# Layer 1's FFN with the turn of each conditioning slot's sums one tile later in the order

## The reference

```python
mod_x = (s_c @ w_mod[l] + b_mod[l])[:, None, :]
sa_x, ca_x, ga_x, sf_x, cf_x, gf_x = jnp.split(mod_x, 6, axis=-1)
...
f_x = _conv_ffn(h_x * (1.0 + cf_x) + sf_x, ffn_w_up[l], ffn_conv_w[l], ffn_conv_b[l], ffn_w_down[l])
h_x = _layer_norm(ALPHA * h_x + gf_x * f_x, ln_g[l, 1], ln_b[l, 1])
...
def _conv_ffn(h, w_up, conv_w, conv_b, w_down):
    u = h @ w_up
    up = jnp.pad(u, ((0, 0), (1, 1), (0, 0)))
    u = up[:, :-2] * conv_w[0] + up[:, 1:-1] * conv_w[1] + up[:, 2:] * conv_w[2] + conv_b
    a, v = jnp.split(u, 2, axis=-1)
    return (jax.nn.silu(a) * v) @ w_down
```

## Time and profile before

| | us |
|---|---|
| median of 3 runs | 2008.89 |
| lowest and highest of them | 2004.92, 2014.71 |
| the profiled execution's own time | 2010.19 |
| its span, first to last instruction | 2008.3 |
| PE busy in the span | 1878.0 |
| DVE busy | 1319.2 |
| POOL busy | 926.3 |
| ACT busy | 889.2 |

### The profile page before, as it was taken

One profiled execution on the slowest core, in us unless ns is written; L12 is line 12 of the kernel. 1 busy time (PEld: TensorE's weight loads), 2 busy tenths in 40 slices (PEclk: granted clock), 3 DMA queues, 4 the chain that ended last, 5 costly groups with the idle time before them and its releaser, 6 DMA issues.

```text
span 2008.3 us, 32378 instructions
## 1 busy us (share of the span) xinstructions
PE 1878.0 (94%) x12286; PEld 1589.9 (79%) x12286; DVE 1319.2 (66%) x2566; ACT 889.2 (44%) x1909; POOL 926.3 (46%) x770
## 2 busy tenths in 40 slices
PE   7899899999999999999999989989899888988997
PEld 4788798767778888888888878888777767877886
DVE  3248999676675977888625366989576754255545
ACT  3224678577443222222433344648377333323542
POOL 3145467111344345554633345766153544754743
PEclk9899799999999999999999999999999999999999
DMA  8563001310111322332221131011401122322321
GB/s 357 201 245 112 22 22 33 110 44 2 64 42 63 122 89 105 126 105 105 84 74 63 42 116 52 34 43 54 152 2 44 63 84 105 105 105 84 126 98 71
DMA packets 29546, 179.38 MB, mean 89 GB/s; under 512 B 3024, under 2 KB 6224, under 8 KB 10320
## 3 DMA queue, kind: packets, MB, share of 16 engines
q1 hardware_dynamic: 22976, 158.16, 21.7%
q10 hardware_dynamic: 6416, 19.14, 2.6%
HBM read 172.05 MB, written 5.24 MB: 88 GB/s over the span
## 4 chain that ended last, share of the span: by engine, by line
PE 66%; DVE 22%; issue 4%; ACT 3%; POOL 2%; DMA 2%; ACTq 1%; DVEq 0%; SPq 0%; POOLq 0%
PE PS L1276 20%; PE PS L1171 18%; PE PS L887 8%; DVE W L1706 6%; PE PS L881 4%; PE PS L1109 3%; PE PS L1133 3%; PE PS L1020 2%; DMA WR<-in_weights 2%; DVE W L1704 2%; PE PS L1093 2%; DVE U L1941 2%; DVE W L2050 1%; PE PS L816 1%; PE PS L1099 1%
## 5 line engine op out<-in xcount | busy, mean ns | idle before, releaser
L1276 PE MATMUL PS<-XH,WS 128*128 128x512 f32 x2016 | 545.3, 357 | 0.9 <-POOL WS L2437 0.9
L1276 PEld LDWEIGHTS PS<-XH,WS 128*128 128x128 f32 x2016 | 361.5, 191 | 55.7 <-POOL WS L2437 1.3
L1276 PE MATMUL PS<-XL,WS 128*128 128x512 f32 x1008 | 359.3, 356 | 0.0
L2437 POOL TENSOR_TENSOR WS<-WR,WS 128x1024 fp32r<-128x1024 f32 x88 | 213.4, 2425 | 311.6 <-ACT WS L1578 311.4
L1642 ACT ACTIVATE W<-PS,PR 128x768 f32<-128x768 f32 (+1 forms) x88 | 78.0, 886 | 440.6 <-PE PS L1276 379.8
L2265 DVE SCALAR_TENSOR_TENSOR W<-PS,PR,W 128x511 f32<-128x511 f32 (+1 forms) x132 | 82.9, 656 | 215.3 <-ACT W L1642 215.3
L1276 PEld LDWEIGHTS PS<-XL,WS 128*128 128x128 f32 x1008 | 192.5, 191 | 26.8
L887 PE MATMUL PS<-EU,XH 128*128 128x256 f32 x624 | 190.1, 305 | 5.6 <-issue 4.6
L2373 POOL TENSOR_TENSOR WL<-WR,EU 128x512 fp32r<-128x512 f32 x96 | 129.5, 1375 | 128.7 <-ACT EU L1333 128.7
L887 PE MATMUL PS<-WL,XH 128*128 128x256 f32 x624 | 182.0, 292 | 0.0
L887 PE MATMUL PS<-EU,HL 128*128 128x256 f32 x624 | 182.0, 292 | 0.0
(11 more groups left out here) (220 smaller groups left out, 4191.7 us busy)
## 6 DMA issues: line engine op xcount, KB each, us to landing
WR<-in_weights SPq DMA_DIRECT2D x128, 1024.0 KB, 4.7
U<-in_weights SPq DMA_DIRECT2D x16, 1024.0 KB, 7.8
U<-in_bias ACTq DMA_DIRECT2D x2, 1792.0 KB, 10.1
H<-in_x SPq DMA_DIRECT2D x1, 2048.0 KB, 7.9
H<-in_x ACTq DMA_DIRECT2D x1, 2048.0 KB, 14.9
U<-in_ln_rows ACTq DMA_DIRECT2D x2, 1024.0 KB, 4.6
WR<-in_weights SPq DMA_DIRECT2D x4, 512.0 KB, 3.7
kept<-H ACTq DMA_DIRECT2D x4, 512.0 KB, 2.6
```

The source lines that it names most:

```text
L1276: mm = pe.matmul(PS[u.pos][:, lo:hi], w[:, part, k, :], src[:, k, lo:hi], start=(k == 0 and src is xh3 and part == 0), stop=(k == KT - 1 a ...
L2437: pool.tensor_tensor(ws5[:, u.c % 2, 1], half_slot(u), ws5[:, u.c % 2, 0], ALU.subtract).then_inc(w_low, 1)
```

## The change

In `ups`, after it is filled, each conditioning entry of layer 1 moves two places on, so that it stands behind both halves of the next tile.

```diff
@@ -627,6 +627,9 @@
                 u = Job()
                 u.kind, u.l, u.j, u.key = "mod", int(key[2] >= LATE), key[2], key
                 ups.append(u)
+        for n in range(len(ups) - 3, -1, -1):
+            if ups[n].kind == "mod" and ups[n].l > 0:
+                ups.insert(n + 2, ups.pop(n))
         n_m = 24 + EARLY
         c = 0
         for u in ups:
```

## The result

The changed kernel takes 1981.58 us (median of four runs, 1976.77 to 1987.43) against 2008.35 for the kernel before on the same chip: a ratio of 0.9864, interval 0.9827 to 0.9902. Two later comparisons of the same pair, with more runs of the kernel before, give 0.9877 (0.9858 to 0.9897) and 0.9877 (0.9861 to 0.9893), which is 24.7 us. The profiled execution took 1987.43 us with a span of 1985.6, 22.7 less than before.

What follows compares the result with a forecast made beforehand. PE was taken as the bound, busy 94% of the span, with time to win only at its stalls: 32.9 us removed less 10.2 of new stops gives 22.7, so 2008.89 - 22.7 = 1986.2 us, range 1982 to 1994.

Steps and rivals of the forecast that it cites:

- The stalls and their slow restarts: Layer 1's up side: PE's four waits for DVE's accumulation, 25.7 us, plus 7.2 us of slow matmuls behind them, go.
- (3,0): First half of tile 3: PE waits for weights whose transfer starts after POOL's low part of (2,1); 1.8 us lost.
- (4,0): First half of tile 4: its weights take slot 20's place, given back after the accumulation; PE loses 1.2 us.
- (5,0): First half of tile 5: weights ready at 1658.4, just when PE gets there; nothing lost, or a few tenths.
- (6,0): First half of tile 6: weights wait for slot 21's place, freed after a 14.8 us accumulation; PE loses 2.1 us.
- The unknown cost of the accumulation: Slot 21's accumulation on DVE may be a microsecond shorter with fewer POOL instructions beside it; 2 us more gain.
- The clock behind the short stops: PE's six stops of about 2 us: no clock loss taken; upper end 9 to 13 us of slow restarts.
- rival 1: PE's clock falls in the new short stops; gain about 15.5 us, 1993 us; chance 0.15.
- Rival 2: Weights land later as two transfers share engines; 5 to 9 us lost, about 1993 us; chance 0.08.
- Rivals 3 and 4: 3: PE waits as long elsewhere for DVE, 2009 us, chance 0.03; 4: clock stays low between stops, 2034 us, 0.02.
- The rest of the span is the same: Outside layer 1's up stage, the span stays the same to a microsecond or two; nothing after takes the gain back.

Runs made afterwards that it cites:

- Experiment 7: Kernel before, with POOL's low part of the weights of layer 1's tiles 3, 5, 16 and 18 cut from 1024 to 64 columns: 1980.66 us, ratio 0.9862.
- experiment 3: The change with each conditioning entry moved one place on instead of two: ratio 0.9891 to the kernel before, stage 244.2 us.
- 8: The changed kernel with three more 512-column products on POOL for each of layer 1's tiles 2 and 15: ratio 0.9943 to the kernel before, stage 253.4 us.
- experiment 9: The change with each entry moved one place on instead of two, run again for a second profile: ratio 0.9898 to the kernel before, stage 245.0 us.

## Why the prediction was right or wrong

The forecast was 1986.2 us, with a range from 1982.0 to 1994.0. The first result, 1981.6, lies just under it; the two repetitions, 1983.2 and 1984.5, lie inside. The mechanism was right; one loss in the sum was too large and the range had too little room below. Against the 26.7 us of the stage the gain was forecast 4.0 too small; taken from the forecast's base of 2008.89 that makes 1982.2, inside the range by 0.2, so the scatter of four runs decides on which side of its lower end their median falls.

- *The stalls and their slow restarts, 32.9 us gone.* Right. The wait's row is gone, and the clock is 1.00 in every stretch of the stage in all three profiles of the change. A little was forgotten: the transposes had cost 0.74 us each at the low clock and cost 0.35 now (1673.87 to 1674.22), 1.6 us more for four.
- *(3,0), 1.8 us lost.* Right: 1.76 idle; by the distance of the matmuls it is 2.1 (1614.94 and 96 matmuls make 1636.7, the next starts at 1638.80).
- *(4,0), 1.2 us lost.* Right: 1.36 idle, 1.6 by distance.
- *(5,0), nothing, or a few tenths.* Right: no idle time there, and its first matmuls come 0.2 us late.
- ***(6,0), 2.1 us lost. Wrong, and this is the step that failed.*** It took the accumulation of slot 21 at the 14.8 us of slot 20. It took 10.1, with one low part and one product of POOL beside it (3.9 us) where slot 20's had three and two (9.4 us before). It began about 1 us later than forecast, so slot 21's place was free 3.6 us sooner than in the sum (1664.30 less the 4.0 by which the stage starts later, against 1663.9). With the sum's 8.4 us from there to ready weights tile 6 was ready at 1672.7, and PE came to it at 1674.22. Twice 2.1 makes 4.2 us. With all of this the sum is 32.9 + 1.6 - 2 x 3.7 = 27.1 for a measured stage of 26.7.
- *The unknown cost of the accumulation.* I had named it as open, "a microsecond shorter" with fewer of POOL's instructions beside it. It was 4.7. The rows could have told more: in 14.8 us are 16 instructions, of which a median one takes 0.48 (the trace of before, L1706: 472/484/2645 ns), so about 7 us were something else, and POOL was busy for 9.4 us of them all. Experiment 7 showed that it was POOL. The rows of this case agree with a rule of the Trainium skill, SBUF — State Buffer, in the section on who interferes with whom, that VectorE, in an instruction with two inputs in SBUF, and GpSimd share a pair of ports that the one to start first keeps for its whole instruction: the longest instruction of the accumulation, 2.6 to 2.7 us, is one of POOL's 2.4 and a little. I didn't weigh it.
- *The clock behind the short stops.* No loss taken, and none seen in the change: three profiles with stops of 1.3 to 1.9 us have clock 1.00 throughout. The reason given was weaker than it read, though: the first case of the earlier trace rows has no unbroken matmuls right ahead of its 2.31 us, but two matmuls and, before them, a stop of 0.59 (1253.10 us). But rival 1 is real. It came in experiments 3, 8 and 9, once or twice a profile, behind stops of 1.87, 1.87 and 3.21, and 2.53 us; where it could be measured it took 1.7 us ((3,0) in experiment 3 ran 7.2 us, in experiment 9 5.5). The change had four such stops in each of three profiles and no fall, which doesn't prove that none will come.
- *Rival 2, later weights.* Not seen in the change, where (4,0) came when order of issue said; a part of it, 1.4 us a transfer, seen in experiment 3. *Rivals 3 and 4.* Not seen.
- *The rest of the span is the same.* The stage's gain isn't given back after it: from the first down products to the end of the span go 129.7 us before (2008.3 - 1878.60) and 129.8 now (1985.6 - 1855.84). Ahead of it the profiles differ by up to 10 us with no change at all, which the range should have had room for on both sides. A gain of 27 with the noise of four runs reaches below 1982 easily.

## What to carry to other kernels

Where an in-order engine stops for a product that it need not yet have, count what stands behind it and put as much of it ahead as the wait is long; then look at once for what the stall had covered, since here a better place for the weights was worth 0 us before the change and 8 after it. Don't carry an instruction's duration from one place to another without its neighbours: read the fastest, the median and the slowest of its kind, and ask which engine was at work during the slow ones. When a kernel's spans scatter by more than the effect, measure the stage between two rows that the scatter doesn't reach.

## What the runs showed of the hardware

DVE's accumulation in SBUF slows down with POOL's work beside it, over four stretches by about 0.8 us for 1 us: 9.8 us with 3.6 us of POOL, 16.1 with 11.7. That much of a stall that the profile puts down to DVE being POOL's doing I had not expected. DVE's taps, that read PSUM, took 0.74 to 0.75 us each with POOL busy or not. The clock of PE can fall to 0.50 behind a stop of 1.9 us and stay at 1.00 behind one of 2.7.
